# Weight tiles of the projections and FFNs issued from ScalarE's DMA queue instead of SyncE's, in one inference step of a hybrid decoder

## The chip, the core and the metric

The kernel runs on one core of a Trainium2 chip. The metric is the device time of one execution in microseconds; a profile comes from one execution of its own, whose time stands beside its span. The engines are TensorE (PE; its weight loads are PEld), VectorE (DVE), ScalarE (ACT), GpSimd (POOL) and SyncE (SP). They run their own instruction streams and meet only at semaphores. DMAs are issued by instructions in such a stream; here SP issues nearly all of them.

## The reference

One step of a two-layer decoder on a prompt of 1024 tokens and on 8 samples of one token each, 1032 columns of width 1024 in all. The parts whose weights the change concerns are the input and output projections of both mixers, the query and output projections of the memory attention, and the SwiGLU FFNs:

```python
def rms_norm(x, g, eps=NORM_EPS):
    y = xf * lax.rsqrt(jnp.mean(xf * xf, axis=-1, keepdims=True) + eps)
    return (y * g.astype(jnp.float32)).astype(x.dtype)
def swiglu(h, w_gate, w_up, w_down):
    return (jax.nn.silu(h @ w_gate) * (h @ w_up)) @ w_down
...
    for i in range(DEPTH):
        h = rms_norm(x, g_mix[i])
        # even: p = h @ w_in_ab -> RWKV-7 heads and RG-LRU blocks -> @ w_out_ab
        # odd:  qkv = h @ w_qkv -> stick-breaking attention -> @ w_out
        x = x + mix
        x = x + memory_xattn(rms_norm(x, g_mem[i]), mk, mv, wq_mem[i], qn_mem[i], wo_mem[i])
        x = x + swiglu(rms_norm(x, g_ffn[i]), w_ffn_gate[i], w_ffn_up[i], w_ffn_down[i])
```

All of it is float32, 2816 columns in the FFN's middle (22 tiles of 128).

## The kernel before

The kernel is written by hand as a sequence of phases. A phase opens one block with a stream for each engine and fresh semaphores, and ends with a barrier of all engines, so no engine enters a phase before the others have left the last one. The residual stream lies transposed in SBUF, 8 tiles of 128 x 1032.

Matrix products work on numbers split into two parts: `hi` (the value rounded to the format of the matmul) and `lo` (the rest). A product of a weight tile with the activations is three chains: hi x hi, hi x lo, lo x hi, each over 3 column blocks of 344. Weight tiles come from HBM in two raw buffers used in turn, 512 KB each (1024 float32 in each of 128 partitions, in rows of 128 numbers; 256 KB for `wo_mem` and for the last group of `w_ffn_down`). For tile m the steps are:

- SP issues the load into `raw[m % 2]` (L361 in `project`, L533 in `ffn`), for m >= 2 once `w_low` has reached m - 1, that is, once the low part of tile m - 2, which held this buffer, is made;
- ScalarE makes `w_hi` (L392, L548; the function `high`) when the tile has landed (`w_in`);
- GpSimd makes `w_lo` (L414, L539) and counts `w_low` up;
- TensorE multiplies (L384, L615) once `w_low` has reached m + 1, and counts `product` up.

ScalarE makes the high parts of tiles 0 and 1 in `first_two`, at the start of the phase, and that of tile m + 2 after product m, since it reuses the buffers of tile m.

`project` and `ffn` start in one of two ways. With an RMS norm (`norm_scalar`, L283 to L289): ScalarE squares the eight residual tiles, TensorE sums them over the partitions (L298), then come `first_two`, ScalarE's square root (L286), VectorE's reciprocal (L324), TensorE's spreading (L303), VectorE's scaling (L330), and the split of the normed tiles (ScalarE L289, then VectorE or GpSimd L311). Six phases start like this: `project` for `w_in_ab` (22 tiles), for `wq_mem` in both layers (4 each) and for `w_qkv_sb` (16), and `ffn` in both layers (68 each). Without a norm: `first_two`, then ScalarE makes the high parts of the operands (L403) and VectorE the low ones (L424). Four phases start like this: `w_out_ab` and `w_out_sb` (8 tiles each), and `wo_mem` in both layers (8 each).

The residual (4128 KB) is spilled to HBM while the mixers need its place: SP issues the spill (L365) in the phases of `w_in_ab` and `w_qkv_sb`, and the reload (L363) in those of `w_out_ab` and `w_out_sb`, both behind the loads of tiles 0 and 1. VectorE waits for the reload before it adds the first product; ScalarE waits for the spill before it overwrites the residual's place.

Of the kernel before, what the change touches and what calls it, by code (L numbers as in the profile page):

```python
# [342 lines left out]
def project(nc, g, ps, tiles, kt, x, takes, gains=None, split=None, reload=None, spill=None, squares=None):  # L343
# [7 lines left out]
    with ExitStack() as mem:  # L351
# [3 lines left out]
        with phase(nc, ("w_in", 2), "w_high", "w_low", "product", "taken", "x_high", "x_low", "x_back", *NORM) as (s, block):  # L355
            @block.sync
            def _(sp):
                for m in range(M):
                    if m >= 2:
                        sp.wait_ge(s.w_low, m - 1)  # L360
                    sp.dma_start(raw[m % 2][:, :, :], tiles[m]).then_inc(s.w_in[m % 2], 16)  # L361
                    if m == 1 and reload is not None:
                        sp.dma_start(takes.residual, reload).then_inc(s.x_back, 16)  # L363
                    if m == 1 and spill is not None:
                        sp.dma_start(spill, g.X[:, :, :]).then_inc(s.spilled, 16)  # L365
                if spill is not None:
                    sp.wait_ge(s.spilled, 16)
# [21 lines left out]
            def _(act):  # L389
# [3 lines left out]

                def first_two():
                    for m in range(2):
                        high(m)

                if room:
                    norm_scalar(act, s, g, ps, room, x, NT, first_two)
                else:  # L400
                    first_two()
                    for k, tile in enumerate(split or []):
                        act.activation(x.hi[:, k, :], tile, ACT.Copy).then_inc(s.x_high, 1)  # L403
                for m in range(M):
                    act.wait_ge(s.product, m + 1)
                    takes.scalar(act, s, m, bank3(ps, 3 * (m % 2)))
                    if m + 2 < M:
                        high(m + 2)
# [86 lines left out]
def ffn(nc, g, d, ps, layer, N):  # L495
# [23 lines left out]
    with ExitStack() as mem:  # L519
# [6 lines left out]
        with phase(nc, ("w_in", 2), "w_high", "w_low", "product", "gate_taken", "hid_raw", "hid_high", "hid_low", "added",  # L526
                   *NORM) as (s, block):
            @block.sync
            def _(sp):
                for j in range(NB_FFN):  # L530
                    if j >= 2:
                        sp.wait_ge(s.w_low, j - 1)
                    sp.dma_start(block_of(raw[j % 2], j), source(j)).then_inc(s.w_in[j % 2], 16)  # L533

# [10 lines left out]
            def _(act):  # L545
# [3 lines left out]

                def first_two():  # L550
                    for j in range(2):
                        high(j)

                norm_scalar(act, s, g, ps, room, H, N, first_two)
                for j in range(NB_FFN):
                    kind, f, m = FFN_BLOCKS[j]
                    act.wait_ge(s.product, END_PRODUCT[j])
# [1756 lines left out]
```

## Time and profile before

| | us |
|---|---|
| median of 3 runs | 5056.27 |
| lowest, highest | 5039.42, 5060.1 |
| the profiled execution, its own time | 5051.88 |
| span of that execution, first to last instruction | 5050.2 |
| busy in it: TensorE, its weight loads | 3847.4, 3306.3 |
| busy in it: VectorE, ScalarE, GpSimd | 1936.1, 1157.7, 1236.1 |

The mean granted clock of TensorE in the profiled execution is 0.847 of full speed. A profile's time line counts from the first instruction. A row of a timeline gives the start, the length, the engine, the line in the kernel, the instruction with output and inputs, a count where rows are merged (the length is then that of the whole run), and in brackets how long the engine was idle before and what ended that. SPq and ACTq are DMA-issuing instructions in the streams of SP and ScalarE; their length is that of the issue, not of the transfer. The landing of a DMA is counted from its issue. The rows on which the prediction rests are shown in a section of their own.

### The profile page before, as it was taken

The numbers are of one execution on the slowest core, as the hardware profiler recorded it, in microseconds if no ns is written. First come the engines' busy times: TensorE is split into PE (matmuls) and PEld (weight loads), VectorE is DVE, ScalarE is ACT, GpSimd is POOL, SyncE is SP. The second block draws the span as 40 slices with busy tenths as digits, with TensorE's granted clock in tenths as the row PEclk, the third lists the DMA queues.
The fourth block names the chain that finished last, engine by engine and source line by source line (L and its number), as shares of the span: only waits on it lengthen the run. The fifth ranks groups of instructions, "written<-read, shape, count | busy, mean of one in ns | idle before, by whom it ended". The sixth has DMA issues, their size and how long they took to land. (4 is left out here: it accounts for less than half of the span.)

```text
span 5050.2 us, 67350 instructions
## 1 busy us (share of the span) xinstructions
PE 3847.4 (76%) x28166; PEld 3306.3 (65%) x28166; DVE 1936.1 (38%) x2014; ACT 1157.7 (23%) x1698; POOL 1236.1 (24%) x627
## 2 busy tenths in 40 slices
PE   7961776677778999998883355555477777999998
PEld 6951565575668999997882222222237546999998
DVE  1047455532232111112006978788742143111112
ACT  2122212212132111112102333233241223111111
POOL 2203111111102222222104555555401102222221
PEclk9985777778789999999986667676789868999999
DMA  3100000021101111112104477787762111111111
GB/s 108 46 12 7 7 4 6 4 70 67 67 17 50 48 47 47 46 40 74 46 17 169 169 280 261 281 296 254 272 218 88 46 67 34 47 48 49 47 47 59
DMA packets 296556, 449.51 MB, mean 89 GB/s; under 512 B 23246, under 2 KB 211931, under 8 KB 295752
## 3 DMA queue, kind: packets, MB, share of 16 engines
q1 hardware_dynamic: 295984, 445.18, 25.9%
q8 instruction: 227, 3.72, 0.3%
q14 instruction: 65, 0.53, 0.0%
q10 hardware_dynamic: 280, 0.07, 0.0%
HBM read 420.68 MB, written 24.55 MB: 88 GB/s over the span
## 5 line engine op out<-in xcount | busy, mean ns | idle before, releaser
L1948 POOL TENSOR_TENSOR k_ring<-k_ring,query_rows 128x1024 f32<-128x1024 f32 x192 | 521.2, 2737 | 441.6 <-DMA k_ring<-in_cache_sb_k 441.4
L539 POOL TENSOR_TENSOR w_lo<-w_raw,w_hi 128x1024 fp32r<-128x1024 f32 (+1 forms) x136 | 317.1, 2332 | 1203.1 <-ACT w_hi L548 1203.1
L615 PE MATMUL ps<-h_ffn_hi,w_hi 128*128 128x344 f32 x2112 | 451.1, 322 | 15.6 <-DVE h_ffn_lo L311 11.0
L615 PE MATMUL ps<-h_ffn_lo,w_hi 128*128 128x344 f32 x2112 | 448.9, 321 | 0.0
L615 PE MATMUL ps<-h_ffn_hi,w_lo 128*128 128x344 f32 x2112 | 446.8, 320 | 0.0
L2167 PE MATMUL ps<-v_ring,cache_weights 128*32 128x512 f32 x1024 | 195.5, 840 | 323.8 <-DMA v_ring<-in_cache_sb_v 323.5
L548 ACT ACTIVATE w_hi<-w_raw 128x1024 fp32r<-128x1024 f32 (+1 forms) x136 | 140.6, 1035 | 1232.4 <-PE ps L615 1232.4
L414 POOL TENSOR_TENSOR w_lo<-w_raw,w_hi 128x1024 fp32r<-128x1024 f32 (+1 forms) x78 | 168.5, 2163 | 970.7 <-ACT w_hi L392 970.7
L615 PEld LDWEIGHTS ps<-h_ffn_hi,w_hi 128*128 128x128 f32 x2112 | 356.3, 189 | 21.0 <-issue 9.6
L615 PEld LDWEIGHTS ps<-h_ffn_lo,w_hi 128*128 128x128 f32 x2112 | 358.4, 189 | 0.0
L1965 DVE TENSOR_REDUCE cache_logits<-k_ring 128x16 f32<-128x1024 f32 x256 | 304.4, 1211 | 135.2 <-POOL k_ring L1948 132.9
L615 PEld LDWEIGHTS ps<-h_ffn_hi,w_lo 128*128 128x128 f32 x2112 | 352.7, 188 | 0.0
L579 DVE TENSOR_TENSOR hidden_whole<-ps,silu 128x1032 f32<-128x1032 f32 x44 | 54.3, 1234 | 711.8 <-PE ps L615 711.8
L1973 DVE TENSOR_TENSOR_SCAN unbroken<-unbroken,ones 128x128 f32<-128x128 f32 (+7 forms) x128 | 267.7, 2131 | 74.3 <-ACT unbroken L2047 74.1
L587 DVE TENSOR_TENSOR residual<-ps,residual 128x1032 f32<-128x1032 f32 x96 | 118.3, 1233 | 461.4 <-PE ps L615 461.4
L2167 PEld LDWEIGHTS ps<-v_ring,cache_weights 128*32 128x32 f32 x1024 | 36.3, 178 | 358.0 <-issue 356.4
L615 PE MATMUL ps<-hidden_hi,w_hi 128*128 128x344 f32 x1056 | 223.4, 320 | 4.6 <-DVE hidden_lo L581 4.6
L615 PE MATMUL ps<-hidden_lo,w_hi 128*128 128x344 f32 x1056 | 224.0, 320 | 0.0
L615 PE MATMUL ps<-hidden_hi,w_lo 128*128 128x344 f32 x1056 | 223.8, 320 | 0.0
L2137 PEld LDWEIGHTS ps<-ident,beta 128*128 128x128 f32 x576 | 90.5, 191 | 166.7 <-issue 92.8
L2137 PE MATMUL ps<-ident,beta 128*128 128x128 f32 x576 | 128.0, 374 | 83.4 <-DVE beta L1979 64.8
L615 PEld LDWEIGHTS ps<-hidden_hi,w_hi 128*128 128x128 f32 x1056 | 176.9, 188 | 5.1 <-DVE hidden_lo L581 5.1
(470 smaller groups left out, 7377.8 us busy)
## 6 DMA issues: line engine op xcount, KB each, us to landing
k_ring<-in_cache_sb_k SPq DMA_DIRECT2D x256, 512.0 KB, 5.1
v_ring<-in_cache_sb_v SPq DMA_DIRECT2D x256, 512.0 KB, 5.1
w_raw<-in_w_ffn_gate SPq DMA_DIRECT2D x44, 512.0 KB, 3.9
w_raw<-in_w_ffn_up SPq DMA_DIRECT2D x44, 512.0 KB, 3.9
w_raw<-in_w_ffn_down SPq DMA_DIRECT2D x40, 512.0 KB, 3.5
w_raw<-in_w_in_ab SPq DMA_DIRECT2D x22, 512.0 KB, 3.9
residual_spill<-residual SPq DMA_DIRECT2D x2, 4128.0 KB, 15.1
residual<-residual_spill SPq DMA_DIRECT2D x2, 4128.0 KB, 15.2
```

Of the source, the lines that this page charges most:

```text
L414: pool.tensor_tensor(W[m % 2].lo[:, :, :], raw[m % 2][:, :, :], W[m % 2].hi[:, :, :].bitcast(F32), ALU.subtract).then_inc(s.w_low, 1)
L539: pool.tensor_tensor(block_of(W[j % 2].lo, j), block_of(raw[j % 2], j), block_of(W[j % 2].hi, j).bitcast(F32), ALU.subtract).then_inc(s.w_ ...
L548: act.activation(block_of(W[j % 2].hi, j), block_of(raw[j % 2], j), ACT.Copy).then_inc(s.w_high, 1)
L579: dve.tensor_tensor(split(whole[:, :]), out_of(FIRST_PRODUCT[j]), split(gate[:, :]), ALU.mult).then_inc(s.hid_raw, 1)
L587: dve.tensor_tensor(x, out_of(q), x, ALU.add).then_inc(s.added, 1)
L615: last = pe.matmul(ps[:, (q % slots) * nb + n, 0:w], wp, xp[:, n * w:(n + 1) * w], start=k == 0 and a == 0, stop=k == kt - 1 and a == 2)
L1948: pool.tensor_tensor(kring[:, m % KR, :], kring[:, m % KR, :], qrows[:, b % 2, :], ALU.mult).then_inc(s.pool_prod, 1)
L1965: dve.tensor_reduce(Z[:, b % 2, PAGES - 1 - p:512:PAGES], kring[:, m % KR, :].rearrange("p (h c) -> p h c", c=HD), AX.X, ALU.add).then_inc ...
L1973: dve.tensor_tensor_scan(back, back, g.ones[:, 0:1].to_broadcast([P, W]), 1.0, ALU.mult, ALU.mult).then_inc(s.scanned[h], 1)
L2137: last = pe.transpose(ps[:, t_bank(key), k * P:(k + 1) * P], beta[:, n % 2, h, 512 * c + k * P:512 * c + (k + 1) * P], g.ident[:, :])
L2167: last = pe.matmul(ps[32 * j:32 * j + 32, PV, :], at, vring[:, (m + o) % VR, half * 512:(half + 1) * 512], start=n == 0, stop=n == PAGES / ...
```

## The change

The loads of the weight tiles leave SP's stream and go into ScalarE's, in `project` and in `ffn`. Tiles 0 and 1 are issued at the head of ScalarE's stream, tile 2 at the end of `first_two`, tile m + 3 ahead of ScalarE's wait for product m. A load keeps its condition (`w_low` at m - 1), which ScalarE now waits for. SP keeps only the reload and the spill, which it issues at once when the phase begins.

```diff
--- before.py
+++ after.py
@@ -355,14 +355,10 @@
         with phase(nc, ("w_in", 2), "w_high", "w_low", "product", "taken", "x_high", "x_low", "x_back", *NORM) as (s, block):
             @block.sync
             def _(sp):
-                for m in range(M):
-                    if m >= 2:
-                        sp.wait_ge(s.w_low, m - 1)
-                    sp.dma_start(raw[m % 2][:, :, :], tiles[m]).then_inc(s.w_in[m % 2], 16)
-                    if m == 1 and reload is not None:
-                        sp.dma_start(takes.residual, reload).then_inc(s.x_back, 16)
-                    if m == 1 and spill is not None:
-                        sp.dma_start(spill, g.X[:, :, :]).then_inc(s.spilled, 16)
+                if reload is not None:
+                    sp.dma_start(takes.residual, reload).then_inc(s.x_back, 16)
+                if spill is not None:
+                    sp.dma_start(spill, g.X[:, :, :]).then_inc(s.spilled, 16)
                 if spill is not None:
                     sp.wait_ge(s.spilled, 16)
 
@@ -391,10 +387,19 @@
                     act.wait_ge(s.w_in[m % 2], 16 * (m // 2 + 1))
                     act.activation(W[m % 2].hi[:, :, :], raw[m % 2][:, :, :], ACT.Copy).then_inc(s.w_high, 1)
 
+                def load(m):
+                    if m >= 2:
+                        act.wait_ge(s.w_low, m - 1)
+                    act.dma_start(raw[m % 2][:, :, :], tiles[m]).then_inc(s.w_in[m % 2], 16)
+
                 def first_two():
                     for m in range(2):
                         high(m)
-
+                    if M > 2:
+                        load(2)
+
+                load(0)
+                load(1)
                 if room:
                     norm_scalar(act, s, g, ps, room, x, NT, first_two)
                 else:
@@ -402,6 +407,8 @@
                     for k, tile in enumerate(split or []):
                         act.activation(x.hi[:, k, :], tile, ACT.Copy).then_inc(s.x_high, 1)
                 for m in range(M):
+                    if m + 3 < M:
+                        load(m + 3)
                     act.wait_ge(s.product, m + 1)
                     takes.scalar(act, s, m, bank3(ps, 3 * (m % 2)))
                     if m + 2 < M:
@@ -525,13 +532,6 @@
         room = norm_room(nc, mem, N)
         with phase(nc, ("w_in", 2), "w_high", "w_low", "product", "gate_taken", "hid_raw", "hid_high", "hid_low", "added",
                    *NORM) as (s, block):
-            @block.sync
-            def _(sp):
-                for j in range(NB_FFN):
-                    if j >= 2:
-                        sp.wait_ge(s.w_low, j - 1)
-                    sp.dma_start(block_of(raw[j % 2], j), source(j)).then_inc(s.w_in[j % 2], 16)
-
             @block.gpsimd
             def _(pool):
                 for j in range(NB_FFN):
@@ -547,13 +547,23 @@
                     act.wait_ge(s.w_in[j % 2], 16 * (j // 2 + 1))
                     act.activation(block_of(W[j % 2].hi, j), block_of(raw[j % 2], j), ACT.Copy).then_inc(s.w_high, 1)
 
+                def load(j):
+                    if j >= 2:
+                        act.wait_ge(s.w_low, j - 1)
+                    act.dma_start(block_of(raw[j % 2], j), source(j)).then_inc(s.w_in[j % 2], 16)
+
                 def first_two():
                     for j in range(2):
                         high(j)
-
+                    load(2)
+
+                load(0)
+                load(1)
                 norm_scalar(act, s, g, ps, room, H, N, first_two)
                 for j in range(NB_FFN):
                     kind, f, m = FFN_BLOCKS[j]
+                    if j + 3 < NB_FFN:
+                        load(j + 3)
                     act.wait_ge(s.product, END_PRODUCT[j])
                     if j + 2 < NB_FFN:
                         high(j + 2)
```

How it moves the instructions is seen at two places. The first is ScalarE at the start of the mixer's input projection, a phase with a norm. `w_raw_26` and `w_raw_27` are the two raw buffers, `lru_gate` holds the squares, `rms` the root. Before:

```order
L388 UNCONDITIONAL_BRANCH [waits barrier_Pool_Activation_PE_DVE_SP_release]
L283 ACTIVATE lru_gate<-residual 128x1032 x2
L283 ACTIVATE lru_gate<-residual 128x1032 [waits summed] x6
L392 ACTIVATE w_hi<-w_raw_26 128x1024 [waits w_in0]
L392 ACTIVATE w_hi<-w_raw_27 128x1024 [waits w_in1]
L286 ACT_TABLE_LOAD
L286 ACTIVATE rms<-ps,eps 96x344 [waits summed]
L289 ACTIVATE h_mix_hi<-lru_gate 128x1032 [waits scaled] x8
L447 ACTIVATE rwkv_rows<-ps 128x1032 [waits product]
L392 ACTIVATE w_hi<-w_raw_26 128x1024 [waits w_in0]
```

And now:

```order
L384 UNCONDITIONAL_BRANCH [waits barrier_Pool_Activation_PE_DVE_SP_release]
L393 DMA w_raw_26<-in_w_in_ab 128x8x128
L393 DMA w_raw_27<-in_w_in_ab 128x8x128
L283 ACTIVATE lru_gate<-residual 128x1032 x2
L283 ACTIVATE lru_gate<-residual 128x1032 [waits summed] x6
L388 ACTIVATE w_hi<-w_raw_26 128x1024 [waits w_in0]
L388 ACTIVATE w_hi<-w_raw_27 128x1024 [waits w_in1]
L393 DMA w_raw_26<-in_w_in_ab 128x8x128 [waits w_low]
L286 ACT_TABLE_LOAD
L286 ACTIVATE rms<-ps,eps 96x344 [waits summed]
L289 ACTIVATE h_mix_hi<-lru_gate 128x1032 [waits scaled] x8
L393 DMA w_raw_27<-in_w_in_ab 128x8x128 [waits w_low]
L454 ACTIVATE rwkv_rows<-ps 128x1032 [waits product]
L388 ACTIVATE w_hi<-w_raw_26 128x1024 [waits w_in0]
L393 DMA w_raw_26<-in_w_in_ab 128x8x128 [waits w_low]
```

Two issues stand ahead of the first square, and one, with a wait for GpSimd's first low part, between the high parts and the root with its table load. From then on there is an issue with such a wait ahead of every copy of a product.

The second place is the start of the `w_out_ab` projection, with buffers `w_raw_76` and `w_raw_77`. SP before:

```order
L361 DMA w_raw_76<-in_w_out_ab 128x8x128
L361 DMA w_raw_77<-in_w_out_ab 128x8x128
L363 DMA residual<-residual_spill 128x8256
L361 DMA w_raw_76<-in_w_out_ab 128x8x128 [waits w_low]
L361 DMA w_raw_77<-in_w_out_ab 128x8x128 [waits w_low]
```

ScalarE before:

```order
L392 ACTIVATE w_hi<-w_raw_76 128x1024 [waits w_in0]
L392 ACTIVATE w_hi<-w_raw_77 128x1024 [waits w_in1]
L403 ACTIVATE mix_hi<-rwkv_rows 128x1032 x4
L403 ACTIVATE mix_hi<-lru_gate 128x1032 x4
L392 ACTIVATE w_hi<-w_raw_76 128x1024 [waits w_in0,product]
L392 ACTIVATE w_hi<-w_raw_77 128x1024 [waits w_in1,product]
```

SP now (after two instructions of the loop that ends here, all that it has in this phase):

```order
L654 REGISTER_ALU [waits barrier_Pool_Activation_PE_DVE_SP_release]
L654 COMPARE_AND_BRANCH
L356 UNCONDITIONAL_BRANCH
L359 DMA residual<-residual_spill 128x8256
L95 UNCONDITIONAL_BRANCH
```

ScalarE now:

```order
L393 DMA w_raw_76<-in_w_out_ab 128x8x128
L393 DMA w_raw_77<-in_w_out_ab 128x8x128
L388 ACTIVATE w_hi<-w_raw_76 128x1024 [waits w_in0]
L388 ACTIVATE w_hi<-w_raw_77 128x1024 [waits w_in1]
L393 DMA w_raw_76<-in_w_out_ab 128x8x128 [waits w_low]
L408 ACTIVATE mix_hi<-rwkv_rows 128x1032 x4
L408 ACTIVATE mix_hi<-lru_gate 128x1032 x4
L393 DMA w_raw_77<-in_w_out_ab 128x8x128 [waits w_low]
L388 ACTIVATE w_hi<-w_raw_76 128x1024 [waits w_in0,product]
```

The reload has nothing ahead of it in SP's stream any more. The three issues stand around the high parts in ScalarE's, the third ahead of the operands' high parts (`mix_hi`).

## Rows read from the trace of the kernel before

**Rows 1.** Page: busy us (share of the span) x instructions, by engine.
```profile
PE 3847.4 (76%) x28166; PEld 3306.3 (65%) x28166; DVE 1936.1 (38%) x2014; ACT 1157.7 (23%) x1698; POOL 1236.1 (24%) x627
```

**Rows 2.** Busy by stretch: from:to, length, then busy and instructions, PEclk, DMA, GB/s.
```profile
1600.00:1800.00 200.00, 200.00 (x1270) 200.00 (x1269) 33.29 (x22) 31.94 (x31) 43.20 (x18) 1.00 0.15 46
```

**Rows 3.** Timeline of ScalarE in FFN 0: start, us, engine, line, instruction, idle before.
```profile
1612.54 1.06 ACT L548 ACTIVATE w_hi<-w_raw 128x1024 fp32r<-128x1024 f32 x1 [9.39 <-PE ps L615]
```

**Rows 4.** Timeline, start of FFN 0.
```profile
1524.22 4.64 POOL L539 TENSOR_TENSOR w_lo<-w_raw,w_hi 128x1024 fp32r<-128x1024 f32 x2 [21.96 <-ACT w_hi L548]
...
1526.40 0.54 ACT L286 ACTIVATE rms<-ps,eps 96x344 f32<-96x344 f32 x1
1526.59 0.37 SPq L533 DMA_DIRECT2D w_raw<-in_w_ffn_gate  x1
```

**Rows 5.** Timeline, start of the first query projection.
```profile
1233.23 4.65 POOL L414 TENSOR_TENSOR w_lo<-w_raw,w_hi 128x1024 fp32r<-128x1024 f32 x2 [83.73 <-ACT w_hi L392]
1234.01 0.53 ACT L286 ACTIVATE rms<-ps,eps 96x344 f32<-96x344 f32 x1
```

**Rows 6.** The line of the root (L286): duration ns min/median/max, first and last start.
```profile
L286 ACT ACT_TABLE_LOAD  x4: 1283/1283/1283, 39.3 to 4258.8; - x4
```

**Rows 7.** Timeline, ScalarE's last parameter issue and first table load.
```profile
14.34 0.30 ACTq L190 DMA_DIRECT2D param_rows<-in_qn_mem  x1
...
14.67 1.28 ACT L196 ACT_TABLE_LOAD   x1 [14.67 <-issue]
```

**Rows 8.** Timeline, start of the w_out_ab projection.
```profile
1064.33 1.02 SPq L361 DMA_DIRECT2D w_raw<-in_w_out_ab  x2
1065.40 1.55 SPq L363 DMA_DIRECT2D residual<-residual_spill  x1
...
1069.99 4.66 POOL L414 TENSOR_TENSOR w_lo<-w_raw,w_hi 128x1024 fp32r<-128x1024 f32 x2 [76.75 <-ACT w_hi L392]
1070.56 1.06 ACT L392 ACTIVATE w_hi<-w_raw 128x1024 fp32r<-128x1024 f32 x1 [0.64 <-DMA w_raw<-in_w_out_ab]
...
1072.60 6.58 DVE L424 TENSOR_TENSOR mix_lo<-rwkv_rows,mix_hi 128x1032 fp32r<-128x1032 f32 x4 [10.20 <-ACT mix_hi L403]
...
1075.89 1.20 PE L384 MATMUL ps<-mix_hi,w_hi 128*128 128x344 f32 x3 [18.28 <-DVE mix_lo L424]
```

**Rows 9.** Timeline, start of the w_out_sb projection.
```profile
3798.18 1.02 SPq L361 DMA_DIRECT2D w_raw<-in_w_out_sb  x2
...
3803.98 1.06 ACT L392 ACTIVATE w_hi<-w_raw 128x1024 fp32r<-128x1024 f32 x1 [0.64 <-DMA w_raw<-in_w_out_sb]
```

**Rows 10.** DMA traffic from 1064 to 1081 us.
```profile
DMA packets 3324, 5.84 MB, mean 344 GB/s; under 512 B 58, under 2 KB 3195, under 8 KB 3195
```

**Rows 11.** Weight tile issued at 1072.4, behind the reload: its landing.
```profile
L361 SPq DMA_DIRECT2D w_raw<-in_w_out_ab x1: 368/368/368, 1072.4 to 1072.4; - x1
...
DMA to landing us min/median/max: 9.8/9.8/9.8
```

**Rows 12.** Spill and reload of the residual: the reload's issues, the landing of all four.
```profile
L363 SPq DMA_DIRECT2D residual<-residual_spill x2: 926/1240/1554, 1065.4 to 3799.2; - x2
...
DMA to landing us min/median/max: 14.6/15.2/15.5
```

**Rows 13.** Timeline, start of the wo_mem projection of layer 0.
```profile
1459.53 1.26 POOL L414 TENSOR_TENSOR w_lo<-w_raw,w_hi 128x512 fp32r<-128x512 f32 x1 [20.14 <-ACT w_hi L392]
...
1461.29 3.91 ACT L403 ACTIVATE mem_out_hi<-mem_q 128x1032 fp32r<-128x1032 f32 x4
```

**Rows 14.** Timeline, starts of the mixer's and of the qkv projection.
```profile
27.97 1.03 SPq L361 DMA_DIRECT2D w_raw<-in_w_in_ab  x2
...
40.63 0.54 ACT L286 ACTIVATE rms<-ps,eps 96x344 f32<-96x344 f32 x1
...
2299.61 0.99 SPq L361 DMA_DIRECT2D w_raw<-in_w_qkv_sb  x2
...
2311.59 0.54 ACT L286 ACTIVATE rms<-ps,eps 96x344 f32<-96x344 f32 x1
```

## The prediction

> **What bounds the kernel now.** First the page's shares: TensorE is busy 3847.4 us of 5050.2 [rows 1]. So the question is what it waits for, and that differs by stretch. The busy times by stretch show the FFN's steady part: 200.00 of 200 us at a granted clock of 1.00 [rows 2]; nothing there costs anything unless it makes TensorE wait. The timeline of ScalarE in the same place shows its cover: it makes its high part of a weight tile after 9.39 us of idleness, released by a product [rows 3]. Then I read the starts of the ten weight phases, where TensorE has nothing to do until the first operands exist. Six begin with an RMS norm (input mixer, query projection twice, qkv, FFN twice), four with a split of operands already there (`w_out_ab`, `w_out_sb`, `wo_mem` twice). There the chain runs through ScalarE, and the change puts work on ScalarE exactly there.
>
> **Steady part: 0.** Of the 214 loads (22 + 8 + 2x4 + 16 + 8 + 2x8 + 2x68 tiles), the 184 from the fourth tile on of their phase run beside products; they move from SP to ScalarE. An issue takes 0.37 us on SP [rows 4], and I take the same for ScalarE. It stands behind `w_high` of tile m+2 and waits for GpSimd's low part of that tile: `w_low` m+2. GpSimd needs 4.64/2 = 2.32 us for one [rows 4]. So ScalarE stands still for about 2.3 us and issues for 0.4 inside an idle time of 9 us. Behind that wait are only the next product's copy, SiLU or high part, all of them after the next product. The load is issued under the same condition as before (the low part of the tile that held the buffer), so it lands no later. If that cover were gone, 184 x 0.37 = 68 us would be the price.
>
> **Norm starts: +17.5.** Before the first square ScalarE now issues tiles 0 and 1. SP's pair takes 1.02 us [rows 8]: +1.0, and all the squares shift by it. Then, after both high parts, tile 2 is issued, which waits for `w_low` 1. In the first query projection GpSimd starts the low parts at 1233.23 and has the first at 1235.55; the root starts at 1234.01 [rows 5]. Now the low part is ready at 1235.55 + 1.02 = 1236.57, with the issue 1236.57 + 0.37 and some 0.1 between instructions: root at 1237.05, **+3.04**. In four of the six phases a table load of 1.28 us stands before the root [rows 6]; there the issue goes in front of it. FFN 0: low part at 1524.22 + 2.32 + 1.02 = 1527.56, issue to 1527.97, table load to 1529.25, root instead of at 1526.40 [rows 4]: **+2.85**. Behind the root are the reciprocal, the spread and the scaling, one after another, and TensorE's first product needs them: all of it is on the path. 4 x 2.85 + 2 x 3.04 = 17.5. That ScalarE's issues hold its arithmetic can be seen once: its last parameter issue ends at 14.64, its first table load begins at 14.67 [rows 7].
>
> **Split starts without a reload (`wo_mem`, twice): +1.2.** The first low part starts at 1459.53 and takes 1.26; the operands' copies start at 1461.29 [rows 13]. The low part is thus there before both high parts are made; only the issue counts, 0.4 in layer 0. In layer 1 both tiles come closer together, so I take up to 1.0 there, 0.6 as mean.
>
> **Reload starts (`w_out_ab`, `w_out_sb`).** ScalarE's own part is nearly free: VectorE's first four low parts take 6.58 us, where the usual 1.23 each would be 4.9, because the first gets through only when GpSimd's pair has ended at 1069.99 + 4.66 = 1074.65; TensorE starts at 1075.89 [rows 8]. A copy one microsecond later meets the same end. What matters is the transfer. Before, SP put tiles 0 and 1 ahead of the 4128 KB reload in one queue; now the reload starts at once on SP's queue, beside the two tiles on ScalarE's. The trace has no stretch with two busy queues, so I bound the delay. From below, 0: the tiles go first. With bytes shared equally, the 1.05 MB of both tiles would let as much of the reload pass: at 344 GB/s over this stretch [rows 10] 3.05 us. From above: tiles end last. The reload is issued 1.07 us after the phase's start and lands 15.2 us later [rows 8, 12], so all bytes are in after 16.3 us. The nearest row is the third tile, the one tile that loads beside a reload now: behind it, it takes 9.8 us to land [rows 11]. And the reload travels in large pieces: of the 3324 packets in 17 us all but 129 are under 8 KB [rows 10]; 4128 KB in 128 pieces is 32 KB each, against 0.5 KB pieces of a weight tile. If the engines serve the two queues piece by piece in turn, the tiles get almost nothing until the reload is through. I take the upper bound for this. `w_out_ab`: second high part at 1064.33 + 16.3 = 1080.6 instead of 1070.56 [rows 8]; from there the low part (1.06 + 0.07 + 2.33) and VectorE's 1.23 lead to TensorE after 4.7 us, where it is 5.33 now: **+9.4**. `w_out_sb`: 3798.18 + 16.3 = 3814.5 instead of 3803.98 [rows 9], less 0.6: **+9.9**. Together +19.3.
>
> The Trainium skill (DMA: Bandwidth & Descriptors, Queues, rings and completion order) says that each DMA engine goes round its queues and changes only at the end of a packet; by it the sum would be the one I take, if a 32 KB piece is one packet, and no run here shows it yet. The same page (Issuing engines are not separate DMA queues) holds that issuing from a second engine saves only issue time: it speaks against any gain here.
>
> **Spill starts (mixer, qkv): +7.8.** The same collision, but the squares cover 9 us of it. Second tile in at 27.97 + 16.3 = 44.3; high part 1.06, issue 0.4, table load 1.28: root at 47.0 instead of 40.63, +6.4, of which 2.85 is counted already: +3.6. qkv: 2299.61 + 16.3 + 2.74 = 2318.6 instead of 2311.59 [rows 14], +7.0: +4.2 more. With bytes shared equally the second tile lands before the squares end: 0.
>
> **Sum.** 17.5 + 1.2 + 19.3 + 7.8 = 45.8 us on the profiled execution's 5051.88 gives 5097.7; I say 5097. The median of the runs shown is 5056.27, 4.4 above that execution. Half a per cent, about what a measurement of this kernel can tell from no change, is 25.3 us: the line is 5081.6.
>
> **Rivals.**
> A (forecast), 5097, chance 0.52.
> B, not slower by half a per cent: the tiles share bytes fairly with the reload or go first. The place is the landing of tile 1 in `w_out_ab`, the price 2 x 3.05, and the spills cost nothing: 17.5 + 1.2 + 6.1 = 24.8, 5076.7 (5070.6 if the tiles are not slowed at all). It decides if tile 1 lands within about 9 us. For it: tile 0 starts with the reload, not behind it. Against: the sizes of the pieces. 0.28.
> C: ScalarE's issue and its wait don't hold its arithmetic; then 18.7 go, and only the collisions stay: 5058 (shared) to 5079. Against: [rows 7]. 0.07.
> D: an issue on ScalarE is dearer, 1 us instead of 0.37. Three in each of ten starts are 30 x 0.63 = 19 more: 5116; in the steady part it is still covered by 9 us. Against: a small issue there ends within 0.30 us [rows 7], though with far less to write down. 0.11.
> E, faster: the third tile no longer stands behind the reload, in the 5.8 us or so of tile 1 instead of 9.8 [rows 11]. It would decide only if the first product ended before 1082.2, but TensorE starts it at 1075.89 and ScalarE's idle time before such a product's end is over 9 us [rows 3]. Price 0, chance 0.02.
>
> **How the numbers follow.** Slower by over 0.5%: nearly all of A and D and a quarter of B, 0.67. Within: most of B and C and a little of A, 0.30. Faster: 0.03. The range goes from inside B's case without slowing, 5067, to the lower side of D, 5112.
>
> **What would show it.** In the profile after: the root of each norm start 2.8 to 3.1 us later after its phase's start, and GpSimd's low part named as what ended ScalarE's wait; the FFN's stretches still 200 of 200; tile 1 of `w_out_ab` landing some 15 us after its issue instead of 5.8 (issued near 1064.8, waited for until 1070.56 [rows 8]); ScalarE's issues at 0.37 us. I am wrong if tile 1 lands within 9 us (then B), if a row shows an issue near 1 us (D), or if TensorE shows idle time inside the FFN's steady part.

## The result, and the profile after

| | before | after |
|---|---|---|
| median of 6 runs each, us | 5052.53 | 5086.20 |
| lowest, highest | 5039.42, 5060.10 | 5083.86, 5099.35 |
| profiled execution, its own time | 5051.88 | 5085.79 |
| span | 5050.2 | 5084.1 |

The change makes the kernel slower by 0.8%: ratio 1.0076, with a 95% interval of 1.0058 to 1.0094. That is 33.7 us by the medians and 33.9 us by the two profiled executions. I had forecast 5097 with a range of 5067 to 5112; it came out 11 us below the forecast and inside the range.

The page first, against [rows 1]: TensorE is busy 75% of the span, and there are now two queues with traffic of this kind. q10 is ScalarE's, with the 106 MB of the weight tiles; q1 is SP's.

```profile
PE 3832.9 (75%) x28166; PEld 3300.4 (65%) x28166; DVE 1922.8 (38%) x2014; ACT 1159.3 (23%) x1698; POOL 1244.9 (24%) x627
...
q1 hardware_dynamic: 108240, 339.26, 18.6%
q10 hardware_dynamic: 188024, 105.99, 7.0%
```

Then what I had named as signs. The FFN's steady part, against [rows 2]: still 200.00 of 200 at 1.00.

```profile
1600.00:1800.00 200.00, 200.00 (x1269) 200.00 (x1268) 34.29 (x22) 31.38 (x31) 40.77 (x17) 1.00 0.16 48
```

The issues at L393, with the transfers' landing below them: the median issue is 0.374 us, the longest, which is the second of a pair, about 0.6. Landing, over all loads of that line, has a median of 3.8 us but a maximum of 16.1.

```profile
L393 ACTq DMA_DIRECT2D w_raw<-in_w_in_ab x22: 374/374/627, 27.1 to 273.4; - x22
...
DMA to landing us min/median/max: 2.6/3.8/16.1
```

The timeline at the start of FFN 0 after the change, against [rows 4]: 

```profile
1528.09 0.38 ACTq L553 DMA_DIRECT2D w_raw<-in_w_ffn_gate  x1
1528.49 0.61 ACTq L553 DMA_DIRECT2D w_raw<-in_w_ffn_up  x1
1529.15 2.02 ACT L283 ACTIVATE squares<-residual 128x1032 f32<-128x1032 f32 x2 [14.49 <-issue]
...
1538.94 4.64 POOL L539 TENSOR_TENSOR w_lo<-w_raw,w_hi 128x1024 fp32r<-128x1024 f32 x2 [22.91 <-ACT w_hi L548]
1541.32 0.37 ACTq L553 DMA_DIRECT2D w_raw<-in_w_ffn_gate  x1
1541.72 1.28 ACT L286 ACT_TABLE_LOAD   x1 [1.91 <-POOL w_lo L539]
```

The reader sees the three steps of the prediction: the pair of issues ahead of the squares (1.01 us from 1528.09), GpSimd's low parts from 1538.94, and the third issue at 1541.32, as soon as the first of them is there. ScalarE's 1.91 us of waiting ahead of the table load is put down to `w_lo`. The line of the root says the same for all six norm starts: ScalarE waits for GpSimd every time.

```profile
  POOL w_lo L421: 6.3, 4
  POOL w_lo L539: 3.8, 2
```

The start of `w_out_ab`, against [rows 8]:

```profile
1067.70 1.06 ACTq L393 DMA_DIRECT2D w_raw<-in_w_out_ab  x2
1067.75 0.36 SPq L359 DMA_DIRECT2D residual<-residual_spill  x1
1082.19 1.06 ACT L388 ACTIVATE w_hi<-w_raw 128x1024 fp32r<-128x1024 f32 x1 [25.94 <-DMA w_raw<-in_w_out_ab]
1083.32 4.65 POOL L421 TENSOR_TENSOR w_lo<-w_raw,w_hi 128x1024 fp32r<-128x1024 f32 x2 [86.65 <-ACT w_hi L388]
1083.80 1.06 ACT L388 ACTIVATE w_hi<-w_raw 128x1024 fp32r<-128x1024 f32 x1 [0.55 <-DMA w_raw<-in_w_out_ab]
1085.70 0.37 ACTq L393 DMA_DIRECT2D w_raw<-in_w_out_ab  x1
1086.12 2.02 ACT L408 ACTIVATE mix_hi<-rwkv_rows 128x1032 fp32r<-128x1032 f32 x2 [1.26 <-POOL w_lo L421]
1087.21 5.28 DVE L431 TENSOR_TENSOR mix_lo<-rwkv_rows,mix_hi 128x1032 fp32r<-128x1032 f32 x4 [21.39 <-ACT mix_hi L408]
...
1089.21 1.20 PE L380 MATMUL ps<-mix_hi,w_hi 128*128 128x344 f32 x3 [28.17 <-DVE mix_lo L431]
```

Both loads and the reload are issued within 1.1 us. ScalarE's first high part waits until 1082.19, its second until 1083.80, and TensorE starts at 1089.21, 21.8 us after the phase's start at 1067.41; before, it was 11.9 us (1075.89 after 1064.02). The landing of the two tiles, against the 5.8 us or so of before, and that of the reload:

```profile
DMA to landing us min/median/max: 14.5/15.0/15.6
```
```profile
L359 SPq DMA_DIRECT2D residual<-residual_spill x2: 332/345/358, 1067.7 to 3817.7; - x2
...
DMA to landing us min/median/max: 12.4/12.6/12.8
```

The tiles are 0.5 MB each, and they land after the 4.1 MB of the reload, though issued in the same microsecond. The DMA traffic of the first 12 us of this phase, 1067 to 1079, shows why:

```profile
DMA packets 241, 4.29 MB, mean 358 GB/s; under 512 B 0, under 2 KB 112, under 8 KB 112
...
q1 hardware_dynamic: 128, 4.23, 87.4%
q10 hardware_dynamic: 112, 0.06, 1.6%
```

In that time SP's queue moved 128 packets and ScalarE's 112, nearly one for one; but a packet of the residual holds 33 KB (4.23 MB / 128) and one of a weight tile 0.5 KB (0.06 MB / 112). The tiles got 1.6% of the engines' time against 87.4%. Their bytes come in only when the residual's are through. By the rule of the Trainium skill that I weighed (DMA: Bandwidth & Descriptors, Queues, rings and completion order: an engine goes round its queues and changes at the end of a packet) the packet here is one contiguous piece; the trace agrees, with these 128 against 112, and with 109 against 109 from 1070 to 1078.5 us, where both queues have work all the time. The same section gives some 9 to 17 descriptors as typical for a packet; no such grouping shows in these counts, and the measurement decides.

**Where the time lies.** The barriers cut a span into 38 phases, so I compared their lengths, phase by phase (last barrier to next barrier, in the profiled executions):

| phase | before, us | change, us | forecast |
|---|---|---|---|
| mixer (`w_in_ab`, spill) | 283.19 | +6.63 | +6.4 |
| `w_out_ab` (reload) | 107.28 | +10.10 | +9.4 |
| query projections | 77.14, 76.97 | +2.77, +2.93 | +3.04 each |
| `wo_mem` | 58.41, 58.16 | +0.09, +0.37 | +0.4, +0.8 |
| FFNs | 785.30, 785.25 | +2.86, +3.00 | +2.85 each |
| qkv (spill) | 214.37 | +8.26 | +7.0 |
| `w_out_sb` (reload) | 106.98 | +10.51 | +9.9 |
| the ten together | 2553.05 | **+47.5** | +45.8 |
| the 28 others, which the change does not touch | 2497.0 | **-13.6** | 0 |

So in the profiled executions my sum was right to 1.7 us where the change works, and the whole miss lies in phases whose instructions are the same. Of the -13.6, 4.1 us are in the eight memory heads, 4.1 in the attention loop, 1.4 each in the query norms and the pair phases, 1.0 in the shift rows. Each profile is of one execution, though, and this one is the second shortest of six; experiment 5 comes back to that.

### The profile page after: what moved, and what is told of

The parts are those of the page before. It is cut to its first block and busy times, and to the rows that moved or that the text cites. A ratio compares the mean times of both kernels' runs of the same rounds, so it can differ in the third digit from the quotient of the medians.

```text
span 5084.1 us, 67350 instructions
## 1 busy us (share of the span) xinstructions
PE 3832.9 (75%) x28166; PEld 3300.4 (65%) x28166; DVE 1922.8 (38%) x2014; ACT 1159.3 (23%) x1698; POOL 1244.9 (24%) x627
## 5 line engine op out<-in xcount | busy, mean ns | idle before, releaser
L625 PE MATMUL ps<-h_ffn_hi,w_hi 128*128 128x344 f32 x2112 | 451.2, 322 | 15.3 <-DVE h_ffn_lo L311 10.8
L2067 ACT ACTIVATE att_t<-ps 128x512 f32<-128x512 f32 (+2 forms) x192 | 90.6, 491 | 398.5 <-PE ps L2147 396.8
## 6 DMA issues: line engine op xcount, KB each, us to landing
residual_spill<-residual SPq DMA_DIRECT2D x2, 4128.0 KB, 12.9
residual<-residual_spill SPq DMA_DIRECT2D x2, 4128.0 KB, 12.6
```

Source lines behind the costliest of these rows:

```text
L625: last = pe.matmul(ps[:, (q % slots) * nb + n, 0:w], wp, xp[:, n * w:(n + 1) * w], start=k == 0 and a == 0, stop=k == kt - 1 and a == 2)
L2067: take(act.activation(attT[:, h, 512 * c:512 * c + w], ps[:, t_bank(key), 0:w], ACT.Copy), key)
```

## The experiments

There were ten runs, two of them without an edit. Two things were to be told apart. First, what the +47.5 is made of. Second, what the -13.6 is: scatter, something systematic in the change (S in the expectations), such as SP having been freed of the loads, or TensorE's clock (C), which is granted at other moments once the program is shifted. "The ten" and "the others" mean the phases of the table above, always against the first profile of before.

**1. The kernel before, again.** No edit.

> The kernel before once more, profiled a second time. The two profiles so far differ by +47.5 us over the ten weight phases and by -13.9 us over the 28 phases that the change does not touch. Theory N (the untouched phases vary from execution to execution): this profile differs from the first one by 5 to 15 us over those 28 phases, and the attention loop and the memory heads vary most. Theory S (the change moves time there): they agree with the first profile within 3 us, and the 14 us belong to the change.

Ratio 1.001 (1.000 to 1.002). The ten +0.5, the others +0.6 (the load of the inputs +1.1, the attention loop -0.9, the heads -0.1). So these two profiles agree within some 1 us, phase by phase. Both are of executions from the middle of the kernel's range, though (5051.88 and 5052.97, where six executions ran from 5039 to 5060 us), so they do not show how far the other phases move between executions.

**2. Only the starts stay on SP.** From before: tiles 0 to 2 of each phase by SP, with spill or reload behind tile 1 as before, and all the later ones by ScalarE.

```diff
-                for m in range(M):
+                for m in range(min(M, 3)):
...
                 for m in range(M):
+                    if m + 3 < M:
+                        load(m + 3)
                     act.wait_ge(s.product, m + 1)
```

> Tiles 0, 1 and 2 of each phase issued by SP as before (reload and spill behind tile 1), all later ones by ScalarE. Theory: all of the loss sits in the starts; the ten phases take what they took before (within 1 us in sum), ratio to before 1.000. Rival S: -14 us of the untouched phases belong to the loads being off SP; then about 5039, ratio 0.997. Rival 2 (184 issues in the steady part cost something): the FFN phases longer by 0.37 us x 65 = 24 us each, ratio 1.01 or more.

Ratio 1.0004 (0.9993 to 1.0015); the ten +0.12, the others -1.65; both FFNs within 0.01 us of before. 184 of the 214 loads have moved and cost nothing: the steady part is 0, as forecast, and all of the loss is in the starts. Nor is anything gained, so no part of the -13.6 is seen to come from these loads having left SP.

**3. Residual behind the first two tiles again.** From after: SP waits until both tiles have landed.

```diff
+                if reload is not None or spill is not None:
+                    sp.wait_ge(s.w_in[0], 16)
+                    sp.wait_ge(s.w_in[1], 16)
```

> The changed kernel, with SP waiting until tiles 0 and 1 have landed before it issues the reload or the spill. Theory (turn by turn between the two queues starves the tiles): tile 1 lands within 6 us again, the w_out_ab and w_out_sb phases lose 10.1 and 10.5 us, the mixer and qkv phases 3.7 and 5.4: 30 us off, about 5057. Rival (a load issued from ScalarE is slow by itself there): tile 1 still lands after 10 us or more and the time stays at 5086.

Ratio 1.0036 (1.0024 to 1.0047). The timeline of the same start in this kernel:

```profile
1068.07 1.02 ACTq L396 DMA_DIRECT2D w_raw<-in_w_out_ab  x2
1072.23 1.06 ACT L391 ACTIVATE w_hi<-w_raw 128x1024 fp32r<-128x1024 f32 x1 [15.58 <-DMA w_raw<-in_w_out_ab]
...
1073.91 1.06 ACT L391 ACTIVATE w_hi<-w_raw 128x1024 fp32r<-128x1024 f32 x1 [0.63 <-DMA w_raw<-in_w_out_ab]
1073.95 0.36 SPq L362 DMA_DIRECT2D residual<-residual_spill  x1
...
1079.25 1.20 PE L383 MATMUL ps<-mix_hi,w_hi 128*128 128x344 f32 x3 [17.84 <-DVE mix_lo L434]
```

The tiles are there 4.2 and 5.8 us after the issue, and TensorE starts 11.5 us after the phase's start at 1067.78. The ten are at +18.2: `w_out_ab` -0.2 and `w_out_sb` +0.3 instead of +10.1 and +10.5, mixer +3.2 and qkv +3.0 instead of +6.6 and +8.3. The overlap of residual and tiles thus costs 29.3 us; that much is shown. The total fell by less (5067.75 against the 5057 I expected), because the others are only at -1.1 here: the heads kept their -4.1, but the attention loop took 6.2 us more than before.

**4. Third load behind the root, or behind the operands.** From after, for all ten phases; here `project`.

```diff
                     for m in range(2):
                         high(m)
-                    if M > 2:
-                        load(2)
...
                         act.activation(x.hi[:, k, :], tile, ACT.Copy).then_inc(s.x_high, 1)
+                if M > 2:
+                    load(2)
                 for m in range(M):
```

> The changed kernel, with tile 2 issued after the norm (or after the operands' high parts), not inside first_two. Theory (ScalarE's wait for the first low part stands in front of the root): the root of each of the six norm starts comes about 1.9 us earlier, 11 us in all, less in the two with a spill where landing sets the pace (about 0.4 each): 8 to 11 us off, 5076. Rival (only the two issues ahead of the squares count): no change.

Ratio 1.0082 (1.0065 to 1.0099). In its first query projection ScalarE no longer waits between the high parts and the root:

```profile
1237.85 1.01 ACTq L393 DMA_DIRECT2D w_raw<-in_wq_mem  x2
...
1247.89 1.99 ACT L388 ACTIVATE w_hi<-w_raw 128x1024 fp32r<-128x1024 f32 x2
...
1249.01 4.64 POOL L421 TENSOR_TENSOR w_lo<-w_raw,w_hi 128x1024 fp32r<-128x1024 f32 x2 [84.52 <-ACT w_hi L388]
1249.78 0.53 ACT L286 ACTIVATE rms<-ps,eps 96x344 f32<-96x344 f32 x1
```

The ten are at +38.3, 9.2 less than after: the wait for `w_low` 1 costs 1.3 to 2.0 us in each norm start but the mixer's (the wait is gone there too, but the tiles came later in this profile: the second high part began 17.4 us after the phase's start instead of 15.9), and what is left of the query projections and FFNs, 0.8 to 1.3, is the first pair of issues. The total did not move, since the others are at only -5.3 here. After that the second question was the more pressing one.

**5. The change, again.** No edit.

> The changed kernel, profiled a second time. Ten weight phases: +47.5 us against the kernel before, as in its first profile (within 1). The 28 others were -13.9 us. If they are tied to the moments at which TensorE is granted its full clock, and those to the program's own course, they come out at -9 to -16 again; if they are chance, anywhere from -14 to +5.

Ratio 1.0089 (1.0072 to 1.0106). The ten +47.1: that repeats. The others are at -10.8, but not in the same places: the heads give -2.3 now and the attention loop -6.4.

What the others do in general stays open, because of which executions were profiled. The change's ten executions fall into two groups, five from 5083.86 to 5088.14 us and five from 5094.55 to 5099.35, and both profiles are of the lower group. With +47.5 in the ten phases and nothing given back, the first profile of before would lead to 5099.4; so in the upper group the others give back 0 to 5 us, not 11 to 14. The ratios say the same: 1.0076 and 1.0089 are 38 and 45 us, with intervals of 29 to 47.5 and 36 to 53.5, and the 47.5 of the ten phases lies at the end of the first and inside the second. No execution of the upper group was profiled.

**6. The delays without the change.** To the kernel before, where SP does all loading, copies of ones into a tile not yet in use are added on ScalarE at eight starts (6.6 us in the mixer, 2.9 in the query projections and the FFNs, 8.3 in qkv, 10.1 in the two reload phases). They delay what the change delays, and do nothing else.

```diff
+        act.activation(flat[:, 0:c], g.ones[:, 0:1].to_broadcast([P, c]), ACT.Copy).then_inc(s.held, 1)
+        act.wait_ge(s.held, count)
...
                 if room:
+                    hold(act, s, g, x.lo[:, :, :], HELD[M] - 0.2)
                     norm_scalar(act, s, g, ps, room, x, NT, first_two)
```

> The kernel before, all loads on SP, nothing of the change; ScalarE is only kept busy at eight starts, in chained copies that nobody needs, for about as long as the change delays those starts: 6.6 us in the mixer, 10.1 in w_out_ab and w_out_sb, 2.9 in both query projections and both FFNs, 8.3 in qkv, 46.7 us in all. Theory C (the other phases gain only because they are shifted against the moments of the clock grants): the memory heads shorten from 17.3 to 16.7 us as in the changed kernel, the 28 other phases sum to -6 or less, the time is 5075 to 5092. Rival (the change itself speeds them up, by keeping SP free): the heads stay at 17.3 and the time is 5095 to 5100.

Ratio 1.0082 (1.0065 to 1.0098). The ten +45.0, the others -6.5 (attention -4.4, values -2.0, heads -1.4, load +2.0). The sum is in the expected range, but the heads are not: I had expected them to shorten as in the changed kernel, and only two of the eight took the 16.7 us or so that seven take there (one does in the kernel before). So the heads do not follow from the delays alone, and since the sum over the others goes from -13.6 to +5.9 us over these profiles (+5.9 in experiment 10), the -6.5 is no proof either.

**7. Edits 3 and 4 together.**

> The changed kernel with both repairs: reload and spill wait for tiles 0 and 1, tile 2 is issued after the norm or the high parts. Theory: the ten phases keep only the 1.0 us of the two first issues in six norm starts, 6 to 8 us in sum against the kernel before (18.2 with the first repair alone, of which the wait for the low part is 11.4). The total may differ from that by the clock's +-10 us: 5045 to 5068. Rival (something else of ScalarE's issues costs): the ten phases keep 12 us or more.

Ratio 1.0016 (1.0007 to 1.0026); the ten +7.8, the others +1.8. The two waits are nearly all that the change costs; the rest is the first pairs of issues, 0.7 to 1.3 us in each norm start but FFN 0's, which kept 2.6. There TensorE starts 1.05 us later than before, and the other 1.5 came while it multiplied; why is not known.

**8. Small pieces for the residual.** From after: the spill's tensor in HBM is laid out so that a row of a partition is 32 pieces of 1032 B instead of one of 33 KB.

```diff
-    aps["spill"] = nc.dram_tensor("residual_spill", (P, DT, NT), F32, kind="Internal").ap()
+    aps["spill"] = nc.dram_tensor("residual_spill", (32, P, DT * NT // 32), F32, kind="Internal").ap().rearrange("c p n -> p c n")
```

> The changed kernel, but the residual's copy in HBM laid out so that spill and reload move in pieces of 1032 bytes (4096 of them) and not of 33 KB (128). Theory (the engines take a piece from each queue in turn, so the size of the pieces sets the shares): beside 1 KB pieces, the 128 pieces of 512 bytes that an engine has for tiles 0 and 1 are through when half the reload is, tile 1 lands after 9 to 12 us, not 15.5; w_out_ab and w_out_sb lose 4 to 7 us each. Rival (a transfer that is issued first, or the larger one, is served first, whatever its pieces): tile 1 still lands after 15 us. The reload itself may get slower with small pieces; VectorE needs it only after the first product.

Ratio 1.0064 (1.0047 to 1.0081). The DMA traffic of this kernel from 1069 to 1081 us, the same stretch of `w_out_ab`:

```profile
DMA packets 4544, 3.60 MB, mean 300 GB/s; under 512 B 32, under 2 KB 4543, under 8 KB 4543
...
q1 hardware_dynamic: 2463, 2.54, 69.7%
q10 hardware_dynamic: 2080, 1.05, 32.0%
```

Again near one for one, 2463 packets against 2080, but now one is 1.0 KB and the other 0.5. From 1072 to 1080 us, where both queues have work all the time, it is exactly one for one:

```profile
q1 hardware_dynamic: 1726, 1.78, 70.8%
q10 hardware_dynamic: 1726, 0.88, 40.3%
```

All of the tiles' 1.05 MB is in before the stretch ends, where it was 0.06 MB. ScalarE's high parts start at 1076.69 and 1081.55, 8.5 and 13.3 us after the phase's start at 1068.21, instead of 14.8 and 16.4. The ten fall by 11.8 us, to +35.7 (mixer +3.4, `w_out_ab` +6.5, qkv +4.9, `w_out_sb` +7.3), though the residual itself lands later, after 19.9 (spill) and 18.3 us (reload) instead of 12.9 and 12.6. Tile 1 landed 12.6 us after its issue, just outside the 9 to 12 that I expected, and the two reload phases gave back 3.6 and 3.2 us. Nothing was changed but the size of the residual's pieces and, with it, its layout in HBM, and the tiles' share followed it.

**9. A small delay.** The kernel before with 1.5 us of such copies in each query projection, to see whether three microseconds of delay are paid at all.

```diff
                 if room:
+                    if M == 4:
+                        hold(act, s, g, x.lo[:, :, :], 1.3)
```

> The kernel before; only in the two query projections ScalarE makes one copy that nobody needs ahead of the first square, which delays these phases by 1.5 us each, 3.0 in all. Theory C (the untouched phases follow from when the full clock comes after a phase's start): in the memory heads of the kernel before it comes 6.3 to 7.7 us after the start, now 1 to 1.5 us sooner; six or more of the eight heads shorten by 0.5 to 1.0, the query norms by some 0.5: 4 to 7 us less there, so the kernel with the delay is no slower, 5046 to 5052 where the kernel before gives 5050. Rival (these phases don't follow from the shift): heads unchanged, +3 us, 5053.

Ratio 0.9997 (0.9988 to 1.0006). The ten +2.6, the others -6.0 (values -2.6, heads -1.5, attention -1.1). No loss shows in the total, but the test is too coarse for it: the interval reaches up to 3 us, which is the whole delay. Of the eight heads two became shorter by 0.6 us, one by 0.5, and one longer by 0.7, so my expectation that most would be shortened missed.

**10. The other way round: operands first.** From before, in the starts without a norm: ScalarE makes the high parts of the first four operands (three for `wo_mem`) while the tiles still load, and only then those of the tiles.

```diff
-                    first_two()
                     for k, tile in enumerate(split or []):
+                        if k == 4 or k == kt - 1 and kt == 4:
+                            first_two()
                         act.activation(x.hi[:, k, :], tile, ACT.Copy).then_inc(s.x_high, 1)
```

> The kernel before, but in the four starts without a norm ScalarE makes the first four (wo_mem: three) high parts of the operands while it waits for tile 0, and only then those of tiles 0 and 1. This looks for a kernel faster than both. In w_out_ab TensorE starts 11.6 us after the phase's start; tile 1 landed after 6.2, with its high part, low part (2.3 behind the first one's 2.3) and no operand left to wait for it could start after 10.3, in wo_mem after some 5 instead of 7. Theory: 1.2 to 1.5 us less in each of the two large ones and 1.5 to 2 in the two small, 5 to 7 us in all, ratio 0.999. Rival (VectorE's low parts of the operands slow GpSimd's low parts of the tiles, since one of the two always waits): no gain, ratio 1.000.

Ratio 0.9976 (0.9966 to 0.9987), median 5039.58: faster than both kernels. Its start of `w_out_ab`:

```profile
1062.71 3.92 ACT L404 ACTIVATE mix_hi<-rwkv_rows 128x1032 fp32r<-128x1032 f32 x4 [11.41 <-PEq L97]
...
1063.78 1.26 SPq L363 DMA_DIRECT2D residual<-residual_spill  x1
1063.80 4.67 DVE L425 TENSOR_TENSOR mix_lo<-rwkv_rows,mix_hi 128x1032 fp32r<-128x1032 f32 x4 [2.99 <-ACT mix_hi L404]
1066.94 1.06 ACT L392 ACTIVATE w_hi<-w_raw 128x1024 fp32r<-128x1024 f32 x1 [0.31 <-DMA w_raw<-in_w_out_ab]
...
1068.68 1.06 ACT L392 ACTIVATE w_hi<-w_raw 128x1024 fp32r<-128x1024 f32 x1 [0.68 <-DMA w_raw<-in_w_out_ab]
...
1070.73 0.79 PEld L384 LDWEIGHTS ps<-mix_hi,w_hi 128*128 128x128 f32 x3 [15.10 <-POOL w_lo L415]
```

The four copies run in the 4.2 us before the first tile is there, in which ScalarE stood idle before. What TensorE waits for last is now named as GpSimd's low part where [rows 8] has VectorE's. It starts 8.3 us after the phase's start at 1062.40 instead of 11.9. The four phases give -3.5, -2.7, -3.0 and -2.4, 11.6 us together, more than the 5 to 7 I expected. Over the executions the kernel gains 11 to 13 us; its profile, which is of the longest of the eight (5047.80), gains 4, since FFN 0 took 1.5 us more there and the attention loop 6.4, neither of them touched by the edit.

## Why the prediction was right, and where it was off

- **Steady part 0: shown.** Experiment 2: 184 loads on ScalarE, the ten +0.12 us. 200.00 of 200 in the FFN window.
- **Norm starts +17.5: right.** +2.77, +2.93, +2.86, +3.00 where no residual moves, and +3.16 and +3.02 in the mixer and qkv once it is out of the way (experiment 3): 17.7. The split into a pair of issues (1.0) and a wait for the low part (1.9) is in the timeline, and experiment 4 takes the second away.
- **`wo_mem` +1.2: +0.5.** In layer 0 the copies of the operands start 5.95 us after the phase's start (1475.38 - 1469.43) where it was 5.54, so the issue holds them for the forecast 0.4; but VectorE's first three low parts then take 3.5 us where they took 3.7, and TensorE starts only 0.2 later.
- **Reload starts +19.3: +20.6, the mechanism shown.** I had taken the upper bound, tiles last. The tiles landed after 14.5 and 15.6 us of a forecast "some 15"; experiment 3 (waiting) and 8 (pieces) take it away and scale it. The size was short because I gave the path from the start of the second high part to TensorE 4.7 us; it took 5.4 (1083.80 to 1089.21), as before (5.3). I had let GpSimd make the second low part at once, but the first tile's high part had begun only 1.6 us earlier, so both low parts run in one piece from 1083.32 to 1087.97 and VectorE's first one gets through only then. The operands' copies behind the third load are not the cause: in experiment 4, without that load ahead of them, the path takes 5.3 too.
- **Spill starts +7.8: +9.2**, counting what lies above 2.85. The mixer was 3.8 for 3.6; qkv 5.4 for 4.2. In qkv the second high part started at 2332.83, 16.7 us after the phase's start, again the whole residual's time. The term that was short is the third load's wait: behind the second tile I counted its high part and the issue (1.5 us), and not the wait for the first low part. Here the first low part ran from 2332.40 to 2334.72, so the issue began at 2334.78; that is 0.9 us more in qkv, and by the same reckoning 0.7 in the mixer.
- **Everything else 0: not so in the profiled executions.** The sum took for granted that phases without a moved instruction keep their length. In the first profile they gave back 13.6 us, and that is why its time was 5086 and not 5097; five of the change's ten executions took 5095 to 5099. Four of the result's six executions were of the lower group, and so is its median. No term of the sum stood for a give-back, so that the range held it is luck.

The rivals: B (shared by bytes, 5076.7) is refuted as a mechanism, by 14.5 and 15.6 us of landing, although the total came within 10 us of its time. The total alone would not have told A from B. C (issues do not hold ScalarE's arithmetic) is refuted by the 1.91 us before the table load. D (dear issues): 0.37 us, at most 0.6 for the second of a pair. E (a gain from the third tile) did not show anywhere.

**What the 13.6 us are.** The heads are the part that can be read. In a memory head TensorE works for its first microseconds at the lower clock of 1.2 GHz, a granted share of 0.50, and then at 2.4 GHz. The first 6.00 us of the first head and its remainder, before and after (the third number from a row's end is the granted clock):

```profile
1385.85:1391.85 6.00, 4.21 (x10) 2.86 (x11) 2.98 (x11) 2.74 (x7) 0.40 (x1) 0.50 0.00 0
1391.85:1403.60 11.75, 8.94 (x55) 7.05 (x53) 5.53 (x22) 6.50 (x20) 0.00 (x0) 0.93 0.00 0
```
```profile
1401.95:1407.95 6.00, 4.21 (x13) 2.85 (x14) 3.12 (x12) 2.77 (x7) 0.40 (x1) 0.56 0.00 0
1407.95:1418.68 10.73, 7.89 (x54) 5.99 (x52) 5.39 (x22) 6.33 (x20) 0.00 (x0) 1.00 0.00 0
```

Before, the first 6 us are all at 0.50 and the other 11.75 at 0.93; if only the two levels occur, the full clock came after 6 + 11.75 x 0.07 / 0.5 = 7.6 us. After the change the first 6 us have 0.56 and the rest 1.00: it came after 6 x 0.44 / 0.5 = 5.3 us. The same instructions then take 16.73 us instead of 17.75. The first two heads as a whole, before and after:

```profile
1385.85:1403.60 17.75, 13.15 (x64) 9.91 (x64) 8.50 (x33) 9.24 (x26) 0.40 (x1) 0.78 0.00 0
1403.60:1421.11 17.51, 12.75 (x64) 9.48 (x64) 8.46 (x33) 9.25 (x26) 0.40 (x1) 0.80 0.00 0
```
```profile
1401.95:1418.68 16.73, 12.10 (x64) 8.85 (x64) 8.51 (x33) 9.10 (x26) 0.40 (x1) 0.84 0.00 0
1418.68:1435.42 16.74, 11.71 (x64) 8.72 (x64) 8.47 (x33) 9.35 (x26) 0.40 (x1) 0.90 0.00 0
```

Over the eight heads of all twelve profiles, those with a mean of up to 0.83 took 17.1 to 17.8 us and those with 0.84 or more 16.7 to 16.9, without exception. That a head's length goes with the clock granted in it is shown. What changes the grant is not: the number of short heads was one in both profiles of before and in experiments 2, 7 and 10, two in 4, 6 and 9, four in 8, seven in 3, and seven and then four in two profiles of the same changed kernel. And the heads are 4.1 of the 13.6 us, 2.3 of the 10.8. For the attention loop the clock explains nothing that I can show, and TensorE is busy for only about half of it: it took 1106.90 us at 0.71 before (the first row below) and 1102.77 at 0.72 after, but 1113.32 at 0.72 in experiment 10 (the second).

```profile
2691.14:3798.04 1106.90, 584.77 (x3456) 288.99 (x3456) 877.35 (x648) 370.36 (x641) 545.78 (x208) 0.71 0.68 243
```
```profile
2685.97:3799.29 1113.32, 572.65 (x3456) 288.12 (x3456) 878.92 (x648) 371.03 (x641) 545.77 (x208) 0.72 0.68 242
```

What else moves it stays open; nothing was tried inside that loop. Nor was it tried what sets the moment of the grant, so I could not forecast the -13.6 us of that profile phase by phase even now.

## What to carry to other kernels

Do not let a transfer in large contiguous pieces start on a second queue beside tiles in small ones that the next step waits for: keep them in order in one queue, or wait for the tiles; it cost 29 us in four starts. A wait placed in an engine's stream holds everything behind it, so put it behind the step that the others need (9 us here), and fill an idle time before the tiles land with work that needs no tile (12 us gained). Where an effect is under half a per cent, compare the lengths of the phases and not only the total, and look at several executions before you explain one profile: here untouched phases came out from 13.6 us shorter to 5.9 us longer in single profiles.

## What the runs showed of the hardware

Two queues with work share the DMA engines packet by packet, whatever a packet holds: 128 of 33 KB against 112 of 0.5 KB in 12 us, and 2463 of 1.0 KB against 2080 of 0.5 KB. I had given that a chance of 0.52, and 0.28 to a share by bytes or the tiles going first. What I had not expected: in the profiled execution of the change, 48 us of delay cost 34; 4 of the 14 that are missing go with a higher granted clock in the memory heads, the rest stays open, and so does how much of it other executions show, five of ten having taken 5095 to 5099 us.
